# Last stage of a one-layer encoder: row scaling and final weight joined on VectorE, residual add moved to GpSimd

## What is computed

```
picked = y_rows[dest].reshape(n, TOP_K, d)
out = einsum('nk,nkd->nd', topw, picked)        # two expert rows per token, weighted
x = x + gt2[:, None] * out                      # gate per channel, residual
return rms_norm(x, g_final)                     # x * rsqrt(mean(x*x) + eps) * g_final
```

## Time and profile before

| what | value |
|---|---|
| median of 3 runs | 2835.71 us (2835.24 to 2836.84) |
| the profiled execution, its own time | 2834.63 us |
| its span, first to last instruction | 2831.8 us |
| mean granted TensorE clock | 0.969 |
| PE, DVE, ACT, POOL busy | 93%, 60%, 54%, 32% of the span |
| chain that ended last, by engine | PE 74%, DVE 8%, issue 7%, DMA 6%, ACT 3% |
| last stage, from its first matmul to the last instruction | 2761.73 to 2831.8 us |

### The profile page before, as it was taken

How to read it: one execution, slowest core, us unless ns; L and a number is a source line. 1 busy time by engine, 2 the same in 40 slices (tenths; PEclk the granted TensorE clock), 3 DMA queues, 4 the chain that set the end, 5 groups by cost and what they waited for, 6 DMA issues and landing times.

```text
span 2831.8 us, 44994 instructions
## 1 busy us (share of the span) xinstructions
PE 2642.7 (93%) x14049; PEld 2192.3 (77%) x14051; DVE 1690.9 (60%) x2964; ACT 1515.4 (54%) x2813; POOL 911.6 (32%) x748
## 2 busy tenths in 40 slices
PE   4999999999999978999999999389999999999978
PEld 2889989999777756888888888268888888888853
DVE  6777565545777765454512455658775635375856
ACT  6555777766665643444432222157665535375756
POOL 4555555565322213344444111011111111111215
PEclk8999999999999989999999999689999999999989
DMA  6222222111000024343443544279886746486998
GB/s 260 62 64 66 68 63 67 29 29 30 23 21 12 14 72 135 125 140 127 138 140 125 181 150 139 86 277 349 329 312 248 295 145 236 147 322 241 389 391 338
DMA packets 191116, 451.94 MB, mean 160 GB/s; under 512 B 36111, under 2 KB 86327, under 8 KB 188941
## 3 DMA queue, kind: packets, MB, share of 16 engines
q1 hardware_dynamic: 171980, 389.46, 39.0%
q0 software_dynamic: 14400, 52.44, 5.0%
q10 hardware_dynamic: 4608, 8.39, 0.8%
HBM read 380.01 MB, written 70.21 MB: 159 GB/s over the span
## 4 chain that ended last, share of the span: by engine, by line
PE 74%; DVE 8%; issue 7%; DMA 6%; ACT 3%; SPq 1%; POOL 1%; DVEq 0%; ACTq 0%; POOLq 0%
PE bank L1928 16%; PE bank L2232 13%; PE bank L2114 6%; PE bank L2159 4%; PE S_ps L2243 3%; PE E_ps L2243 3%; DMA sb_w_in<-in_w_gate_up 3%; PE S_ps L2114 3%; PE E_ps L2114 3%; PE O_ps L1970 2%; PE S_ps L1958 2%; PE S_ps L2054 2%; PE O_ps L2125 1%; PE S_ps L2125 1%; PE S_ps L2159 1%
## 5 line engine op out<-in xcount | busy, mean ns | idle before, releaser
L822 POOL TENSOR_TENSOR sb_h_lo<-sb_hT,sb_h_hi 128x512 fp32r<-128x512 f32 x256 | 372.2, 1475 | 486.3 <-ACT sb_h_hi L949 486.3
L2232 PE MATMUL bank<-sb_gu,sb_x_hiT 128*128 (+1 forms) x1568 | 494.2, 397 | 11.7 <-DVE sb_x_loT L1800 9.0
L1928 PE MATMUL bank<-sb_w_hi,sb_h_hi 128*128 128x384 f32 x1024 | 363.5, 355 | 1.5 <-DVE sb_hT L1384 0.9
L2232 PEld LDWEIGHTS bank<-sb_gu,sb_x_hiT 128*128 128x128 f32 x1568 | 293.3, 189 | 74.2 <-issue 11.1
L1928 PE MATMUL bank<-sb_w_hi,sb_h_lo 128*128 128x384 f32 x1024 | 343.6, 336 | 0.0
L1928 PE MATMUL bank<-sb_w_lo,sb_h_hi 128*128 128x384 f32 x1024 | 343.3, 335 | 0.0
L1786 DVE TENSOR_TENSOR sb_gu<-sb_w_in,sb_gu 128x1024 f32 (+1 forms) x256 | 300.5, 1220 | 62.2 <-ACT sb_gu L1237 60.3
L867 POOL TENSOR_TENSOR sb_g_lo<-sb_g_raw,sb_g_hi 128x1408 fp32r<-128x1408 f32 x64 | 212.4, 3338 | 333.3 <-ACT sb_g_hi L1111 333.3
L1237 ACT ACTIVATE sb_gu<-sb_w_in 128x1024 f32 (+1 forms) x256 | 256.6, 1059 | 100.7 <-DMA sb_w_in<-in_w_gate_up 75.8
L2232 PE MATMUL bank<-sb_gu,sb_x_loT 128*128 (+1 forms) x784 | 307.3, 392 | 0.0
L1068 ACT ACTIVATE sb_e_sb<-sb_e_sb,sb_o_row 128x256 f32<-128x256 f32 (+2 forms) x320 | 167.2, 525 | 149.2 <-DVE sb_o_row L1509 105.8
(11 more groups left out here) (391 smaller groups left out, 5982.8 us busy)
## 6 DMA issues: line engine op xcount, KB each, us to landing
sb_w_in<-in_w_gate_up SPq DMA_DIRECT2D x256, 512.0 KB, 6.3
sb_w_in<-in_w_expert_down SPq DMA_DIRECT2D x128, 512.0 KB, 5.3
sb_g_raw<-in_w_gb SPq DMA_DIRECT2D x64, 704.0 KB, 4.0
sb_late_w<-in_w_ada SPq DMA_DIRECT2D x64, 256.0 KB, 2.8
sb_yp<-y_d SPq DMA_DIRECT2D x16, 1024.0 KB, 21.4
sb_w_raw<-in_w_qkv SPq DMA_DIRECT2D x112, 96.0 KB, 2.1
sb_x_round<-in_x SPq DMA_DIRECT2D x4, 2048.0 KB, 17.8
sb_hT<-in_w_ada SPq DMA_DIRECT2D x4, 2048.0 KB, 18.0
```

The lines of the kernel that those rows point to most:

```text
L822: nc.gpsimd.tensor_tensor(h_lo[c][:, ks], tile_src(g, T, ks), h_hi[c][:, ks].bitcast(F32), ALU.subtract).then_inc(sem("h_lo_ready"), 1)
L1928: last = nc.tensor.matmul(bank[c][:, 0:PASS_COLS].rearrange("p (a m) -> p a m", a=1), x[c][:, k, :], w[:, ds(row + k, 1), :], start=(k == ...
L2232: last = nc.tensor.matmul(PS[j][:].rearrange("p (a n) -> p a n", a=1), x[:, k, :], gu[:, ds(gu_row(e, part, k), 1), j * DE:(j + 1) * DE], ...
```

## The change

VectorE no longer adds the residual, except for tiles 14 and 15. GpSimd does it for tiles 0 to 13, as soon as a tile has been gated. ScalarE's scaling of the row (`norm_rows`) and GpSimd's product with `gfb` both go: `finish(t)` on VectorE now takes the reciprocal and then multiplies the row by the reciprocal and by `gfb` in one operation (`scalar_tensor_tensor`, "the joint product" below). `finish` stands two tiles behind instead of one. For tiles 14 and 15 the add stays on VectorE, and ScalarE waits for `last_ready` there. SP waits for `out_ready` alone, which VectorE now raises. Nothing else of the program differs.

```diff
--- before.py
+++ after.py
@@ -780,10 +780,7 @@
         for t in range(TT):
             sp.dma_start(yp[t][:], yv[:, t]).then_inc(sem(Y_IN[t][0]), 16)
         for t in range(TT):
-            if t in LAST:
-                sp.wait_ge(sem("last_ready"), t - LAST[0] + 1)
-            else:
-                sp.wait_ge(sem("out_ready"), t + 1)
+            sp.wait_ge(sem("out_ready"), t + 1)
             sp.dma_start(ov[:, t, :], yp[t][:, 0, :]).then_inc(sem("out_stored"), 16)
         sp.wait_ge(sem("out_stored"), 16 * TT)
 
@@ -933,11 +930,10 @@
         pool.wait_ge(sem("xg_in"), 16 * (total + 2))
         pool.sem_inc(sem("experts_done"), 1)
 
-        pool.wait_ge(sem("rows_in"), 112)
-        for t in range(TT):
-            if t not in LAST:
-                pool.wait_ge(sem("normed"), t + 1)
-                nc.gpsimd.tensor_tensor(yp[t][:, 0, :], yp[t][:, 0, :], gfb[:], ALU.mult).then_inc(sem("out_ready"), 1)
+        for t in range(LAST[0]):
+            pool.wait_ge(sem(X1_IN[t // 4][0]), X1_IN[t // 4][1])
+            pool.wait_ge(sem("gated_rows"), t + 1)
+            nc.gpsimd.tensor_tensor(yp[t][:, 0, :], yp[t][:, 0, :], xl[:, t, :], ALU.add).then_inc(sem("acc_ready"), 1)
 
 
     @block.scalar
@@ -1318,22 +1314,18 @@
             last.then_inc(sem("mixers"), 1)
 
         def squares_of(t):
-            act.wait_ge(sem("acc_ready"), t + 1)
+            if t in LAST:
+                act.wait_ge(sem("last_ready"), t - LAST[0] + 1)
+            else:
+                act.wait_ge(sem("acc_ready"), t + 1)
             nc.scalar.activation(yp[t][:, 1, :], yp[t][:, 0, :], ACT.Square, accum_out=ssq3[:, t:t + 1]).then_inc(sem("sumsq"), 1)
             act.wait_ge(sem("sumsq"), 2 * TT + t + 1)
             nc.scalar.activation(rms3[:, t:t + 1], ssq3[:, t:t + 1], ACT.Sqrt, bias=eps_col, scale=1.0 / D).then_inc(sem("rms"), 1)
 
-        def norm_rows(t):
-            act.wait_ge(sem("rstd"), ROUNDS + TT + t + 1)
-            nc.scalar.activation(yp[t][:, 0, :], yp[t][:, 0, :], ACT.Copy, scale=rstd3[:, t:t + 1]).then_inc(sem("normed"), 1)
-
         for t in range(MIXERS):
             weights_of(t)
-        for t in range(TT + 1):
-            if t < TT:
-                squares_of(t)
-            if t >= 1:
-                norm_rows(t - 1)
+        for t in range(TT):
+            squares_of(t)
             if t + MIXERS < TT:
                 weights_of(t + MIXERS)
 
@@ -1837,29 +1829,31 @@
 
         dve.wait_ge(sem("rows_in"), 112)
 
-        def add_residual(t):
+        def gate_rows(t):
             dve.wait_ge(sem("mixed"), t + 1)
             row = yp[t][:, 0, :]
             for j in range(2):
                 half = slice(j * 512, (j + 1) * 512)
                 last = nc.vector.tensor_tensor(yp[t][:, 0, half], PS[2 * (t % MIXERS) + j][:], gt2b[:, half], ALU.mult)
             last.then_inc(sem("gated_rows"), 1)
-            dve.wait_ge(sem(X1_IN[t // 4][0]), X1_IN[t // 4][1])
-            dve.wait_ge(sem("gated_rows"), t + 1)
-            nc.vector.tensor_tensor(row, row, xl[:, t, :], ALU.add).then_inc(sem("acc_ready"), 1)
+            if t in LAST:
+                dve.wait_ge(sem(X1_IN[t // 4][0]), X1_IN[t // 4][1])
+                dve.wait_ge(sem("gated_rows"), t + 1)
+                nc.vector.tensor_tensor(row, row, xl[:, t, :], ALU.add).then_inc(sem("last_ready"), 1)
 
         def finish(t):
             dve.wait_ge(sem("rms"), ROUNDS + TT + t + 1)
             nc.vector.reciprocal(rstd3[:, t:t + 1], rms3[:, t:t + 1]).then_inc(sem("rstd"), 1)
-            if t in LAST:
-                dve.wait_ge(sem("normed"), t + 1)
-                nc.vector.tensor_tensor(yp[t][:, 0, :], yp[t][:, 0, :], gfb[:], ALU.mult).then_inc(sem("last_ready"), 1)
+            dve.wait_ge(sem("rstd"), ROUNDS + TT + t + 1)
+            row = yp[t][:, 0, :]
+            nc.vector.scalar_tensor_tensor(row, row, rstd3[:, t:t + 1], gfb[:], ALU.mult, ALU.mult).then_inc(sem("out_ready"), 1)
 
         dve.wait_ge(sem("rows_in"), 112)
         for t in range(TT):
-            add_residual(t)
-            if t >= 1:
-                finish(t - 1)
+            gate_rows(t)
+            if t >= 2:
+                finish(t - 2)
+        finish(TT - 2)
         finish(TT - 1)
 
 
```

## The result

| | before | after |
|---|---|---|
| median of 7 runs each, same chip | 2835.71 us (2831.18 to 2838.7) | 2849.34 us (2845.0 to 2854.54) |
| ratio, 95% interval | | 1.0048, 1.0039 to 1.0058 |
| span of the profiled execution | 2831.8 us | 2852.0 us |
| end of gate 2 to end of gate 14 | 41.20 us, 3.43 a tile | 57.22 us, 4.77 a tile |
| end of gate 14 to end of the last product | 11.09 us | 9.43 us |

The change makes the kernel 13.6 us slower; 2850.0 was forecast, in a range of 2846 to 2854. The last three lines of the table give 16.02 - 1.66 - 1.33 = 13.0 us of it. The profiled execution of the change took 2854.54 us, the longest of its seven, and its last stage begins late (first matmul at 2768.12 instead of 2761.73), so the two spans should not be subtracted; stretches inside the stage can be.

What follows compares the result with a forecast made beforehand. TensorE bounds the last stage before; VectorE, standing for GpSimd's adds, was to become the bound. 15.9 us lost over 12 periods less 1.6 gained in the tail gives 14.3; 2835.71 + 14.3 = 2850.0 us, range 2846 to 2854.

Steps and rivals of the forecast that it cites:

- The turns: Last stage: each joint product stands until GpSimd's add is over; twelve near 3.4 us, four near 1.29.
- The period: Last stage, gate to gate on VectorE: 4.76 us a tile against 3.43, over 12 periods.
- GpSimd's start behind the gate: Last stage: GpSimd's add starts 0.07 us after the end of VectorE's gate.
- the rest of the product: Last stage: what is left of the joint product after GpSimd's add, 1.10 us, bounded by 0.9 and 1.29.
- the next gate: Last stage: VectorE's gate after the joint product adds 1.21 us to each tile.
- The margin in the race: Last stage, behind each gate: GpSimd's add starts 0.05 us ahead of VectorE's joint product.
- the attention stage's row: Attention stage: GpSimd goes first though 0.03 us behind; VectorE's operation takes 1.88 us instead of 0.74.
- the first rival: Last stage: VectorE goes first or the two don't hinder each other; 2834.1 us, not slower; chance 0.09.
- The tail: End of gate 14 to the last product: 9.51 us instead of 11.08, a gain of 1.6.
- The end: Behind the last product: the store is unchanged, with no gain or loss counted.
- the second rival: Last stage from tile 10: TensorE's waits bring the slow clock, 6.9 us a tile; 2855 us; chance 0.04.
- The third: Last stage: the joint product runs at half speed, 1.10 us more each, 16 on the path; 2867.6 us; chance 0.01.

Runs made afterwards that it cites:

- the add behind: The changed kernel with GpSimd's add of tile t waiting until the joint product of tile t-2 has ended; ratio to before 1.0003.
- the short fill: The changed kernel with a GpSimd fill of 128x8 elements ahead of each add of tiles 2 to 13; ratio to before 0.9984.
- the three kernels in which VectorE goes first: The changed kernel with GpSimd's add delayed by a 128x256 fill, by waiting for VectorE's reciprocal, or by a 128x8 fill; ratios to before 0.9994, 0.9992, 0.9984.
- half an add: The changed kernel with GpSimd adding only columns 0 to 511 of tiles 0 to 13; ratio to before 1.0002.

## Why the prediction was right, step by step

- **The turns.** Joint products of 3.465 were foreseen "near 3.4", twelve of them, with four at 1.284. The runs without the add, with half of it and with the add behind show that nothing but the standing makes them long.
- **The period**, 4.76 forecast, 4.77 measured, is partly luck. GpSimd's start behind the gate is 0.143, not 0.07; the add 2.345, not 2.38; the rest of the product 1.08, not 1.10; the next gate 1.20, not 1.21. The sum is right because the first error is undone by the others.
- **The margin in the race was wrong, and that GpSimd won it is partly luck.** I had GpSimd 0.05 us ahead of the joint product, from the start of an operation without inputs. It is 0.04 behind, and goes first all the same, as in the earlier trace rows, where it was 0.03 behind. So the forecast stood on the attention stage's row and not on the starts, and far closer to the edge than a chance of 0.81 says: the first rival's tipping point, "a joint product some 0.1 us ahead", lies above 0.04 and at most at 0.13 (0.08 by the recorded start behind the short fill), and 0.1 more at the most would have made this rival true, at the 2831 to 2833 us of the three kernels in which VectorE goes first. The rows that the forecast stood on are near an edge too: at 0.032 to 0.036 that pair went either way. The rule that an operation that starts first goes first (the Trainium skill, SBUF — State Buffer, "SBUF: two separate sides") gives the wrong winner here when the starts are taken as the trace records them; that the turns are whole operations agrees, 3.465 against 1.285.
- **The tail** was forecast as 9.51 and took 9.43, from 11.09.
- **The end** was forecast as unchanged ("the store behind the last product is unchanged"). The store is; the program's end was not tied to it but to GpSimd, and 1.33 us were gained. It hides in the median: 14.3 - 1.33 would have been 2848.7, and 2849.34 was measured.
- **TensorE** waits from tile 10 on, for ScalarE's matrices, as said, by 1.07 instead of 1.3 us, at a granted clock of 1.00: the second rival did not come. The third fell with the run without the add.

## What to carry to other kernels

Before work is moved between VectorE and GpSimd, write down when each two-tensor operation on SBUF of the one starts beside those of the other: whichever loses the turn stands for the whole of the other's operation, and the cheap loser is the engine that is not the bound. If both hang on the same event, the winner is decided by hundredths of a microsecond, more finely than recorded starts in another place can tell, and one more wait in GpSimd's list can turn a loss of 0.5% into none. And look at the engine that is done last at the program's end: a late GpSimd operation can close the kernel although all data have landed.

## What was not expected of the hardware

- In the last stage GpSimd wins the turn in all 24 tiles of the change and of half an add, with its recorded start 0.037 to 0.040 us behind VectorE's, and loses it at 0.08 behind a fill and at 0.13. In the attention stage it loses some turns at 0.032 to 0.036, and against a VectorE operation without a column it lost at 0.021 to 0.027.
- GpSimd starts 0.14 to 0.17 us behind the VectorE operation that releases it when it works on two tensors. Of operations without inputs, the fills started 0.12 behind the gate of tile 2, the one in the earlier trace rows after 0.07.
- A fill, which reads nothing, takes no part in the turns: one of 128x256 ran 0.31 us from 0.01 us behind a joint product on, and the product took its 1.285.
- GpSimd is done with its list 8.27 us after its last operation, within 2 ns over eleven profiles.
